# Eight projection columns (beta, decay) as full fp32 products, second in the order of the projection instead of last

## The reference

```python
h = modulate(rms_norm(x, norm1_gain), shift1, scale1)
proj = h @ w_in                      # 256 x 1024 by 1024 x 3592
qa, ka, va, qkv_b, z_b, b_raw, a_raw = jnp.split(proj, cuts, axis=-1)
...
beta = jax.nn.sigmoid(b_raw)         # 4 columns, one for each delta-rule head
g = -jnp.exp(dn_a_log) * jax.nn.softplus(a_raw + dn_dt_bias)   # 4 columns
```

## Time and profile before

| quantity | value |
|---|---|
| median of the timed runs | 1749.46 us (3 runs, 1748.37 to 1753.6) |
| profiled execution, span of its records | 1748.0 us |
| time around the span in the profiled execution | the page gives none; the median lies 1.46 us above the span |
| PE busy | 1619.2 us, 93% of the span |
| DVE busy | 1269.7 us, 73% |
| ACT busy | 876.9 us, 50% |
| stage of the projection, first product of group 0 to the copy L735 | 35.6 to 131.3 us |
| first transpose of the next stage | 131.7 us |

### The profile page before, as it was taken

One profiled execution on the slowest core, in us unless ns is written; L12 is line 12 of the kernel. 1 busy time (PEld: TensorE's weight loads), 2 busy tenths in 40 slices (PEclk: granted clock), 3 DMA queues, 4 the chain that ended last, 5 costly groups with the idle time before them and its releaser, 6 DMA issues. The chain is left out here.

```text
span 1748.0 us, 26003 instructions
## 1 busy us (share of the span) xinstructions
PE 1619.2 (93%) x10132; PEld 1461.1 (84%) x10132; DVE 1269.7 (73%) x2518; ACT 876.9 (50%) x1409; POOL 66.9 (4%) x87
## 2 busy tenths in 40 slices
PE   2998588999999999999999999989999889889989
PEld 2886586799999999997888888888788777789977
DVE  6787866678999799986776777656888566654654
ACT  3423325545544555554555555556456656455443
POOL 0300430000000000000000000020000000000000
PEclk9998698999999999999999999999999899999999
DMA  9746224546676655556777777745443223445543
GB/s 336 263 145 176 101 82 149 176 145 224 224 239 212 212 153 150 158 160 240 243 241 244 240 245 242 258 148 170 141 148 124 92 74 117 139 154 175 187 154 111
DMA packets 114838, 314.40 MB, mean 180 GB/s; under 512 B 10448, under 2 KB 11040, under 8 KB 105248
## 3 DMA queue, kind: packets, MB, share of 16 engines
q1 hardware_dynamic: 103424, 278.09, 48.7%
q10 hardware_dynamic: 10976, 33.63, 5.7%
q0 software_dynamic: 320, 1.06, 0.2%
HBM read 293.86 MB, written 18.89 MB: 179 GB/s over the span
## 5 line engine op out<-in xcount | busy, mean ns | idle before, releaser
L287 PE MATMUL ps<-parts,parts 128*128 128x512 f32 (+1 forms) x5016 | 978.0, 356 | 36.2 <-DVE parts L277 31.1
L287 PEld LDWEIGHTS ps<-parts,parts 128*128 128x128 f32 x5016 | 830.2, 192 | 172.4 <-DVE parts L277 23.6
L272 ACT CAST parts<-lead 128x512 fp32r<-128x512 f32 x940 | 580.4, 621 | 651.2 <-PE ps L287 429.6
L277 DVE TENSOR_TENSOR parts<-lead,parts 128x512 fp32r<-128x512 f32 x940 | 649.9, 698 | 342.1 <-ACT parts L272 337.9
L1505 PE MATMUL ps<-parts,parts 128*128 128x256 f32 x3072 | 385.3, 285 | 4.5 <-DVE parts L277 4.5
L1505 PEld LDWEIGHTS ps<-parts,parts 128*128 128x128 f32 x3072 | 372.6, 192 | 5.5 <-DVE parts L277 5.5
L362 PE MATMUL ps<-lead,mem 128*128 128x128 f32 (+2 forms) x314 | 53.1, 339 | 70.7 <-ACT mem L475 39.5
L362 PEld LDWEIGHTS ps<-lead,mem 128*128 128x128 f32 (+2 forms) x314 | 46.2, 166 | 76.9 <-issue 32.5
L1679 DVE TENSOR_SCALAR mem<-lead,mem 128x128 f32<-128x128 f32 x256 | 71.0, 340 | 0.0
L1491 PE MATMUL ps<-mem 128*128 128x128 f32 x512 | 67.8, 275 | 0.8 <-DVE mem L1679 0.8
L1491 PEld LDWEIGHTS ps<-mem 128*128 128x128 f32 x512 | 62.8, 192 | 1.1 <-issue 1.1
(11 more groups left out here) (323 smaller groups left out, 1072.8 us busy)
## 6 DMA issues: line engine op xcount, KB each, us to landing
lead<-in_peer_expert_down SPq DMA_DIRECT2D x64, 1024.0 KB, 5.6
lead<-in_peer_expert_up SPq DMA_DIRECT2D x64, 1024.0 KB, 5.8
lead<-in_w_in SPq DMA_DIRECT2D x50, 1024.0 KB, 5.1
lead<-in_w_ffn_in SPq DMA_DIRECT2D x22, 1024.0 KB, 5.2
act_spill<-mem ACTq DMA_DIRECT2D x32, 512.0 KB, 5.1
mem<-act_spill ACTq DMA_DIRECT2D x32, 512.0 KB, 3.6
mem<-in_w_ada SPq DMA_DIRECT2D x26, 512.0 KB, 5.1
lead<-in_w_ffn_out SPq DMA_DIRECT2D x11, 1024.0 KB, 4.9
```

Of the source, the lines that this page charges most:

```text
L272: act.copy(w_hi[g % BUFFERS], st.words(n, u * UNIT, UNIT)).then_inc(hi_ready, 1)
L277: dve.tensor_tensor(w_lo[g % BUFFERS], st.words(n, u * UNIT, UNIT), w_hi[g % BUFFERS].bitcast(F32), ALU.subtract).then_inc(lo_ready, 1)
L287: mm = pe.matmul(o, lhs[a], rhs[b], start=start and i == 0, stop=stop and i == 2, skip_group_check=True, **kw)
```

## The change: what it does

The eight columns are no longer made of three fp32r products of split operands. PE multiplies the fp32 rows (`x_full`, the tile `full` with a name of its own) by the fp32 weights `w_ba`, 16 matmuls with 8 moving columns. They stand between group 0 and group 1, behind the tap transposes and the wait for their copy, and write PSUM bank 3, which group 0 leaves free. DVE copies them out at unit 5 of group 1. The cast of the weights (ACT) and their split (DVE) go, with their semaphore. Two waits are new: PE waits before group 4, the first that writes bank 3 again, for that copy, and POOL waits for the 16 matmuls before it writes over `full`.

```diff
@@ gpsimd
+                pool.wait_ge(s_ba, 1)
                 pool.wait_ge(s_bank_v, 2)
                 pool.wait_ge(s_bank_a, 2)
@@ tensor
                         transposes(pe, [(ps[:, 4, 0:48], taps_rows)]).then_inc(s_tap, 1)
                         pe.wait_ge(s_tapo, 1)
+                        pe.wait_ge(s_ba_in, 16)
+                        pe.wait_ge(norm1.s_full, KT)
+                        for tt in range(TT):
+                            for k in range(KT):
+                                mm = pe.matmul(ps[:, 3, tt * 8:tt * 8 + 8], x_full[:, k, tt * P:(tt + 1) * P], w_ba[:, k, :],
+                                               start=k == 0, stop=k == KT - 1)
+                        mm.then_inc(s_ba, 1)
+                    if c == 4:
+                        pe.wait_ge(s_bao, 1)
                     if c >= 2:
                         pe.wait_ge(s_bank_v, c - 1)
                         pe.wait_ge(s_bank_a, c - 1)
                     product_group(pe, c, g0 + KT * c, 0, "f" if 3 <= c < 6 else "t", (x_hi, x_lo), norm1)
-                for tt in range(TT):
-                    for k in range(KT):
-                        ts = slice(tt * P, (tt + 1) * P)
-                        mm = three(pe, ps[:, 7, tt * 8:tt * 8 + 8], [x_hi[:, k, ts], x_lo[:, k, ts]],
-                                   [ba_hi[:, k, :], ba_lo[:, k, :]], k == 0, k == KT - 1)
-                mm.then_inc(s_ba, 1)
@@ vector
-                dve.wait_ge(s_bah, 1)
-                dve.tensor_tensor(ba_lo, w_ba, ba_hi.bitcast(F32), ALU.subtract)
...
+                    if c == 1 and u == 5:
+                        dve.wait_ge(s_ba, 1)
+                        dve.tensor_copy(ba, ps[:, 3, 0:16].rearrange("p (t n) -> p t n", n=8)).then_inc(s_bao, 1)
...
-                dve.wait_ge(s_ba, 1)
-                dve.tensor_copy(ba, ps[:, 7, 0:16].rearrange("p (t n) -> p t n", n=8)).then_inc(s_bank_v, 1)
@@ scalar
-                act.wait_ge(s_ba_in, 16)
-                act.copy(ba_hi, w_ba).then_inc(s_bah, 1)
```

More of the change, by code:

```diff
@@ L572, in build @@
         s_ba, s_bank_v, s_bank_a = sem("proj1_ba_done"), sem("proj1_bank_out_dve"), sem("proj1_bank_out_act")
[L573 to L577, removed]
+        s_z3, s_bao, s_taps, s_tap, s_tapo, s_conv = (sem(n) for n in (
+            "conv_lead_zero", "ba_out", "taps_loaded", "taps_transposed", "taps_out", "conv_steps"))
+        x_full = at(O_B + 4096, KT, S)
+        norm1 = Norm("norm1", h, x, norm_scale, norm_shift, x_full)
         with nc.Block() as block:
```

## The result

The changed kernel is slower: 1759.57 us median (1759.43 to 1764.39, 6 runs) against 1748.91 us of the kernel before (1748.05 to 1753.6, 6 runs). The ratio is 1.0061 with a 95% interval of 1.0048 to 1.0074. I had forecast 1746.2 us, in a range of 1742.5 to 1750.0. The profiled execution took 1759.53 us, with a span of 1757.8.

A forecast was written before the change was run, and what follows sets the result against it. The prediction took PE to set the pace. Its terms, -5.9 (stage end) + 2.9 (new run) - 0.3 (next head) = -3.3 us, off the 1749.5 us median gave 1746.2 us, range 1742.5 to 1750.0.

The forecast's parts named there:

- The end of the stage: Projection's end: without 48 narrow products and one copy it comes 5.9 us earlier, bounds 4.8 to 7.0.
- The new run: Between groups 0 and 1: 32 fp32 instructions 0.11 us apart, 3.5 us; group 1 starts 2.9 us late.
- The rival with four passes: New fp32 matmuls make four passes each, 64 x 0.11 = 7.0 us; total 1749.7 us; chance 0.08, shared with gains lost otherwise.
- The clock in the middle: Around the new fp32 matmuls: possible clock fall mid-stage after about 4.2 us of low work; not in the forecast's sum.
- The rival of the short stretch: Clock falls mid-projection for a short half-clock stretch costing 1.6 us; total 1747.8 us; chance 0.23.
- The head of the next stage: Next stage's 32 transposes at full clock, scores still wait for ACT: only -0.3 us (0 to -0.5).
- The rival on the slow side: Mid-projection, new fp32 matmuls and 10 us of group 1 at half clock: +6.1 us, 1755.6 us; chance 0.04.

The follow-up runs named there:

- copies_first: Changed kernel with ACT's four copies of queries and keys ahead of its large activation: 1756.96 us median, in two groups (1744.90 to 1747.26, 1756.16 to 1761.43).
- dense_mid: Changed kernel with 16 unread products of 512 columns between the scores of the third and fourth head: 1758.05 us, ratio 1.0043 to the kernel before.
- dense_fill: Changed kernel with 10 unread products of 512 columns between the query/key transposes and the attention scores: 1749.37 us, ratio 0.9991 to the kernel before.
- narrow_fill: Changed kernel with 20 unread products of 8 columns between the query/key transposes and the attention scores: 1762.12 us, ratio 1.0058 to the kernel before.
- drop: Kernel before without the eight columns' 48 products, zeros for the beta and decay columns: 1757.79 us, ratio 1.0038 to the kernel before.
- position: Kernel before with its 48 fp32r products, cast and split kept, moved between group 0 and group 1: 1765.94 us, ratio 1.0087 to the kernel before.
- format: Kernel before with 16 fp32 matmuls replacing the 48 products at the stage's end: 1746.49 us, ratio 0.9989; nine times 1744.74 to 1750.12, one 1759.20.
- g4_copies_fill: Changed kernel with ACT's copies first, 6 products of 512 columns before the scores, fp32 matmuls moved into group 4: 1745.42 us, ratio 0.9977 to the kernel before.

## Why the prediction was wrong

Point by point, in the order of its steps:

- **The end of the stage.** Right. The copy of group 6 is the last work, and the next stage starts 0.3 us behind it. Between the two profiles this gave 7.0 us, the upper bound of the term, where 5.9 had gone into the sum. Net of the projection, that stage starts 2.64 us earlier.
- **The new run.** Right to 0.1 us in this execution: 32 instructions at 0.11 us, group 1 2.9 us late. The rival with four passes is refuted for few columns: PE has 32 records and not 64. By the rule that the prediction cites beside it (the Trainium skill, FP8 and Floating Point Precision, TensorE Precision Notes), the run would cost four array passes a matmul; here it costs two weight loads.
- **The clock in the middle.** The rival of the short stretch came true: half clock from before 54 to after 57. From group 1's start (+2.73) to the copy of group 6 (+4.37) it cost 1.6 us, as priced. That is one execution. In the profile of `copies_first`, whose program is the same up to there, the clock fell inside the new run and stayed down until after 58; the run took 5.37 us, group 1 started at 55.13 instead of 53.10, and the copy of group 6 came at 129.92, 1.9 us later than in the profile after:

```profile
49.91 5.37 PE L650 MATMUL ps<-mem 128*128 128x8 f32 x32 [0.30 <-DVE mem L719]
```
- **The head of the next stage.** This is the step that failed: "Without narrow products ahead of them the clock should still be full. But the scores wait for ACT ... Only that wait goes: -0.3 us (0 to -0.5)." The clock was full over the transposes, and the scores' start gained 0.6 us. But I asked only when the scores start and not at which clock they run. Faster transposes in front of a fixed ACT chain mean a longer gap, 2.42 us instead of 0.76, and the clock fell 0.7 us behind it, before the first head of the scores was done. The term was not -0.3 but -0.6 + 12.6 = +12.0 us. The spans differ by the sum: -0.16 ahead of group 0, +2.89 for the run, +1.64 for the short stretch, -7.01 at the end, -0.61 and +12.59 here, and +0.46 behind the scores, together +9.8.
- **The rival on the slow side** had the right mechanism, a long stretch at half clock, in the wrong place, and got a chance of 0.04. Its sentence "dense work brought the clock back in group 0" was true, and `dense_mid` shows the same among the scores; the stage of the attention has no products of 512 columns.

What was in the rows and not read: the clock had risen between 136 and 137, 2 us before the scores started at 138.34. The 16.7 us of the scores hung on that, and the change touched what stood right in front of it. The fall between 160 and 161, near the end of 4.1 us of idle time on PE, showed that a gap can have this price. (The share of 0.61 in that row puts the fall at about 160.2, while PE still stood; the prediction has it at 160.6.)

Shown by runs: the gap's lack of dense products causes the fall (`dense_fill` against `narrow_fill`), and neither the place nor the form of the new products is needed for it (`drop`, `position`). Shown too is that dense work raises the clock and the scores then keep it (`dense_mid`). Open are why the transposes raised it in before and the scores at half clock never did, what decides in one execution between the two outcomes of `copies_first` and `format`, and the price of the stretch in group 1, whose length differs between executions.

## What to carry to other kernels

Where work in front of a wait gets faster, ask what the engine does in the wait and at which clock the next stretch will run, not only when it starts. For every stretch of small or fp32 products, read which clock it has and what ran ahead of it when it got that clock; a change that takes away or speeds up what stands before it can cost the whole stretch. Put narrow products where PE waits for another engine, and between dense ones: in group 4 they cost nothing up to the end of the stage (`g4_copies_fill`).

## What the runs showed of the hardware

- The attention scores hold the clock that they have from their second microsecond on: 16.7 us at 2.4 GHz in the kernel before, 29 us at 1.2 GHz in the kernel after, at a PE busy share of 1.00 in both. Five microseconds of 512-column products took them from one to the other.
- Products of 512 columns are not the only work at which the clock rose: in the kernel before it rose between 136 and 137, and in `format` between 131 and 132, each time with nothing on PE but 128-column transposes since the stage's start (131.66 and 127.48).
- An fp32 matmul of few columns is two instructions and costs two weight loads, 2 x 0.11 us at 2.4 GHz and 2 x 0.21 us at 1.2 GHz (L900); a narrow fp32r product costs one such load. For 8 columns, full fp32 takes two thirds of the time of the three-product form. For 256 columns it is the other way round: at full clock an fp32 matmul of the scores takes 0.62 us (139.15 to 139.77 in the profile before), three fp32r products 0.38 us (12 of them from 95.47 to 96.98 in `g4_copies_fill`).
- The clock column can be wrong early in a profile. In the profile of before it read 1.00 from 36 to 40 us, while products took 628 ns as at half clock; the profile after has 0.50 for the same stretch, with the same six products in two microseconds. First before, then after:

```profile
36.00:38.00 2.00, 2.00 (x6) 1.52 (x6) 2.00 (x6) 2.00 (x5) 0.00 (x0) 1.00 1.05 386
```
```profile
36.00:38.00 2.00, 2.00 (x6) 1.61 (x5) 2.00 (x6) 1.75 (x4) 0.00 (x0) 0.50 1.04 384
```
